# Moving the decay preparation of a recurrence into the stage ahead of it, and half of the output weights to the head of their stage's load queue

## What is computed

```python
f = lb + (1.0 - lb) * jax.nn.sigmoid(hf)                # decay of each token and channel
o, S = hgrn2_scan(silu(hq), 1.0 - f, hi, log(f), S0)    # query, key, value, log decay
...
b = jnp.cumsum(gc, axis=1)                              # summed log decays of a chunk
inter = einsum('bchk,bhkv->bchv', qc * exp(b), S)
S_new = exp(b_last)[..., None] * S + einsum('bshk,bshv->bhkv', kc * exp(b_last[:, None] - b), ic)
...
h = x + mix @ w_out                                     # mix = [attention heads || HGRN2 heads]
```

## Time and profile before

| | |
|---|---|
| median of 3 runs | 3429.63 us (3428.11 to 3436.2) |
| the profiled execution: its own time | 3433.21 us |
| its span in the profile | 3431.4 us |
| PE busy in the span | 3219.1 us (94%) |
| DVE, ACT, POOL busy | 2492.2 us (73%), 1311.3 us (38%), 1023.5 us (30%) |
| mean granted TensorE clock | 0.96 |

### The profile page before, as it was taken

How to read it: one execution, slowest core, us unless ns; L and a number is a source line. 1 busy time by engine, 2 the same in 40 slices (tenths; PEclk the granted TensorE clock), 3 DMA queues, 4 the chain that set the end, 5 groups by cost and what they waited for, 6 DMA issues and landing times. The chain is left out here.

```text
span 3431.4 us, 54854 instructions
## 1 busy us (share of the span) xinstructions
PE 3219.1 (94%) x20435; PEld 1970.3 (57%) x20435; DVE 2492.2 (73%) x5514; ACT 1311.3 (38%) x2581; POOL 1023.5 (30%) x1076
## 2 busy tenths in 40 slices
PE   7999987698899898999999999996999999999997
PEld 4668652575466554666666666653555555555554
DVE  4222562445423489999999999977988888888887
ACT  3000553321200124677776777743222222222222
POOL 0000000000000003899999999952111111111110
PEclk9999998677999999999999999998999999999998
DMA  3220787422422354878888888899788787787774
GB/s 149 98 98 32 271 297 304 164 88 104 169 65 78 126 186 147 278 276 296 298 295 295 279 284 305 294 348 377 288 293 301 281 305 291 291 297 287 294 289 150
DMA packets 213106, 803.43 MB, mean 234 GB/s; under 512 B 33824, under 2 KB 92320, under 8 KB 169088
## 3 DMA queue, kind: packets, MB, share of 16 engines
q1 hardware_dynamic: 176000, 531.81, 42.5%
q0 software_dynamic: 36864, 268.45, 22.4%
HBM read 665.19 MB, written 201.98 MB: 253 GB/s over the span
## 5 line engine op out<-in xcount | busy, mean ns | idle before, releaser
L1692 PE MATMUL psum<-arena 128*128 128x400 f16 x6144 | 1079.8, 334 | 29.4 <-DVE arena L1740 29.3
L2083 PE MATMUL psum<-arena 128*128 128x400 f16 x6144 | 1048.8, 332 | 25.9 <-DVE arena L2129 25.9
L2083 PEld LDWEIGHTS psum<-arena 128*128 128x128 f16 x6144 | 596.1, 97 | 478.6 <-DVE arena L2129 26.3
L1692 PEld LDWEIGHTS psum<-arena 128*128 128x128 f16 x6144 | 592.6, 98 | 444.7 <-DVE arena L1740 33.6
L1664 POOL TENSOR_SCALAR arena<-arena 128x128 f16<-128x128 f16 x800 | 721.6, 915 | 41.0 <-DVEq L1904 24.2
L116 POOL DMA_INDIRECT arena<-in_experts,arena x256 | 286.3, 1118 | 1131.6 <-DVE arena L149 1040.8
L135 ACT ACTIVATE arena<-arena 128x1 f32<-128x1 f32 x256 | 51.5, 201 | 868.0 <-DVE arena L128 867.7
L149 DVE SCALAR_TENSOR_TENSOR arena<-arena 128x1024 f32<-128x1024 f32 x256 | 331.8, 1296 | 21.3 <-issue 9.6
L2136 DVE TENSOR_TENSOR arena<-arena,psum 128x800 f32<-128x800 f32 x256 | 252.1, 985 | 107.3 <-PE psum L2083 107.3
L128 DVE CUSTOM_DVE_ANT_0 arena<-arena 128x1024 f32<-128x1024 f32 x256 | 312.0, 1220 | 19.0 <-DMA arena<-in_experts,arena 18.0
L1955 ACT ACTIVATE arena<-arena 128x128 f16<-128x128 f16 x800 | 246.0, 388 | 86.9 <-DVE arena L1912 86.2
(11 more groups left out here) (241 smaller groups left out, 3425.0 us busy)
## 6 DMA issues: line engine op xcount, KB each, us to landing
arena<-in_u_feat SPq DMA_DIRECT2D x128, 512.0 KB, 7.0
arena<-in_experts SPq DMA_DIRECT2D x128, 512.0 KB, 5.5
scratch_acts<-arena SPq DMA_DIRECT2D x128, 400.0 KB, 5.3
arena<-scratch_gates SPq DMA_DIRECT2D x32, 1600.0 KB, 8.0
arena<-scratch_acts SPq DMA_DIRECT2D x128, 400.0 KB, 6.6
scratch_gates<-arena SPq DMA_DIRECT2D x48, 1024.0 KB, 8.4
out_k_win_sample<-in_cache_k SPq DMA_DIRECT2D x32, 1022.0 KB, 21.5
out_v_win_sample<-in_cache_v SPq DMA_DIRECT2D x32, 1022.0 KB, 21.3
```

The lines of the kernel that those rows point to most:

```text
L1692: last = pe.matmul(psum[:, 2 * p + k, 0:SLD], w[:, s, q, :], xs[:, q, k * SLD:(k + 1) * SLD], start=q == 0 and w is u_hi and xs is x_hi, s ...
L2083: last = pe.matmul(psum[:, 2 * (n % BANKS) + i, 0:SLD], w[:, s, k, q * P:(q + 1) * P], hs[:, s, k, i * SLD:(i + 1) * SLD], start=k == 0 an ...
```

## The change

1. In attend_sample, DVE gets `center_decays()` behind `normalize(1)`: the middles are first copied to tiles of their own, then the sums are centred in place, carries are made, and the sums are clamped. The carries move to a fixed place at the arena's end.
2. ACT makes exp(-centred) for one head group at a time (tile `falling`, which takes the place of `resets`), DVE multiplies that group's keys (`scale_keys(g)`); two groups ahead of `write_out(0)`, two behind it. `copy_turned(1)` stands between groups 1 and 2. Then ACT makes exp(centred) in place and the carries' exponentials, and DVE scales the queries ahead of `write_out(1)`.
3. In hgrn all of that goes, with its waits: PE starts at once with turning the keys. A new `step_dve` 1 only says that the state sum is zeroed.
4. In hgrn SP issues the half of the output weights right behind the first x tile, without a wait, ahead of the second x tile and the seven window copies.
5. In attend_sample SP issues the bias load behind the keys of the first two sequences.

```diff
@@ hgrn, SP
             load_x(0)
+            sp.dma_start(w_half, x["w_out"][:, 0:4, :]).then_inc(w_half_loaded, 16)
             load_x(1)
             shift = SHIFTS_IN + SHIFTS_ATTEND
             for n in range(shift, SHIFTS - 9):
                 shift_window(sp, x, n, windows_shifted)
-            sp.wait_ge(step_dve, 1)
-            sp.dma_start(w_half, x["w_out"][:, 0:4, :]).then_inc(w_half_loaded, 16)
@@ hgrn, ACT
-            act.wait_ge(step_dve, 1)
-            act.activation(ek, eq, ACT.Exp, scale=-1.0).then_inc(step_act, 1)
-            act.drain()
-            act.activation(eq, eq, ACT.Exp)
-            act.activation(carry[:, :, 1:], carry[:, :, 1:], ACT.Exp)
-            act.activation(carry_s, carry_s, ACT.Exp).then_inc(step_act, 1)
...
+            act.wait_ge(step_dve, 1)
             for n in range(NCH):
@@ hgrn, PE
-            pe.wait_ge(keys_scaled, 1)
...
             pe.wait_ge(turn_copied, 9)
-            pe.wait_ge(step_dve, 2)
@@ hgrn, DVE
+            dve.memset(sum_state[:, 0], 0.0)
+            dve.drain().then_inc(step_dve, 1)
             dve.wait_ge(loaded, 16 * 5)
-            (centring of eq, carries, clamp, key and query scaling: L836 to L862)
@@ attend_sample, SP
-            sp.dma_start(bias, x["bias_sample"]).then_inc(constants_loaded, 16)
...
             load_keys(0)
             load_keys(1)
+            sp.dma_start(bias, x["bias_sample"]).then_inc(constants_loaded, 16)
             sp.wait_ge(new_ready, 9)
@@ attend_sample, DVE
+            def center_decays():
+                mid, mid_s = CH // 2 - 1, ST // 2 - 1
+                chunks = f[:, :, 0:SEQ].rearrange("p g (n c) -> p g n c", c=CH)
+                chunks_s = f[:, :, SEQ:T].rearrange("p g (n c) -> p g n c", c=ST)
+                dve.tensor_copy(middle, chunks[:, :, :, mid])
+                dve.tensor_copy(middle_s, chunks_s[:, :, :, mid_s])
+                dve.drain()
+                for g in range(G):
+                    dve.tensor_tensor(chunks[:, g], chunks[:, g],
+                                      middle[:, g].unsqueeze(2).broadcast_to([P, NCH, CH]), ALU.subtract)
+                    dve.tensor_tensor(chunks_s[:, g], chunks_s[:, g],
+                                      middle_s[:, g].unsqueeze(2).broadcast_to([P, SB, ST]), ALU.subtract)
+                dve.drain()
...
+                dve.tensor_scalar(f, f, 40.0, -40.0, ALU.min, ALU.max)
+                dve.drain().then_inc(decay_dve, 1)
+
+            def scale_keys(g):
+                dve.wait_ge(falling_ready, g + 1)
+                dve.tensor_tensor(k[:, g, :], k[:, g, :], falling, ALU.mult).then_inc(keys_scaled, 1)
...
             normalize(1)
+            center_decays()
+            scale_keys(0)
+            scale_keys(1)
             write_out(0)
+            scale_keys(2)
+            scale_keys(3)
+            dve.wait_ge(rising_ready, 1)
+            dve.tensor_tensor(q, q, f, ALU.mult).then_inc(keys_scaled, 1)
             write_out(1)
             dve.wait_ge(out_done, 2 * H)
+            dve.wait_ge(keys_scaled, G + 1)
@@ attend_sample, ACT
             for silu in silus:
                 act.activation(silu, silu, ACT.Silu)
-            copy_turned(1)
+            act.wait_ge(decay_dve, 3)
+            for g in range(G):
+                if g >= 1:
+                    act.wait_ge(keys_scaled, g)
+                act.activation(falling, f[:, g, :], ACT.Exp, scale=-1.0).then_inc(falling_ready, 1)
+                if g == 1:
+                    copy_turned(1)
             act.drain()
+            act.activation(f, f, ACT.Exp)
+            act.activation(carry[:, :, 1:], carry[:, :, 1:], ACT.Exp)
+            act.activation(carry_s, carry_s, ACT.Exp)
+            act.drain().then_inc(rising_ready, 1)
```

More of the change, by code:

```diff
@@ L48 @@
 BIAS0 = WORDS - SEQ
+CARRY0 = WORDS - 4 * (NCH + 1) - 2 * 4 * SB
 ROWS = 2 * P
@@ L185, in build @@
             "row_slots": at(SLOT0, SLOTS, 2 * D), "row_sums": at(SUM0, 2, D), "x_row": at(XROW0, D),
+            "carry": at(CARRY0, G, NCH + 1),
+            "carry_s": at(CARRY0 + G * (NCH + 1), 2, G * SB).rearrange("p a (g b) -> p a g b", g=G),
             "row_index": at(IDX0, 2, P).bitcast(U32), "row_weight": at(WGT0, 2, P),
@@ L589, in hgrn @@
         k = mix[:, 4:8, :]
-        ek = at(word, G, T); word += GT
+        word += SB * 512
         causal = at(word, P); word += P
@@ L594, in hgrn @@
         hnorm = at(word, 1); word += 1
-        carry = at(word, G, NCH + 1); word += G * (NCH + 1)
-        carry_s = at(word, 2, G * SB).rearrange("p a (g b) -> p a g b", g=G); word += 2 * G * SB
+        carry, carry_s = m["carry"], m["carry_s"]
         state = at(word, 4, G, P); word += 4 * G * P
@@ L603, in hgrn @@
         inv = at(word, G * P); word += G * P
-        assert word <= WORDS, word
+        assert word <= CARRY0, word
         eq = at(F0, G, T)
@@ L610, in hgrn @@
         loaded = sem("hgrn_loaded")
-        step_act = sem("hgrn_act")
         step_dve = sem("hgrn_dve")
-        keys_scaled = sem("hgrn_keys_scaled")
         turn_ready = sem("hgrn_turn_ready")
@@ L811, in _ @@
                           masked[0:NS, g, 0:NS], start=g == 0, stop=False, skip_group_check=True)
-            pe.wait_ge(step_dve, 3)
+            pe.wait_ge(step_dve, 2)
             for g in range(G):
@@ L972, in attend_sample @@
         SLOT = 4 * NKEY
-        assert KT * 512 == SLOT and word + 2 * SLOT <= WORDS
+        assert KT * 512 == SLOT and word + 2 * SLOT <= CARRY0
         slot_words = (word, word + SLOT, F0, F0 + SLOT)
@@ L983, in attend_sample @@
         lbt = at(word, 8, G); word += 8 * G
+        q, carry, carry_s, falling = feat[:, FHQ, :, :], m["carry"], m["carry_s"], resets
+        middle = at(word, G, NCH); word += G * NCH
+        middle_s = at(word, G, SB); word += G * SB
         assert word <= F0 + 8 * T
@@ L986, in attend_sample @@
         decay_dve = sem("decay_dve")
+        falling_ready = sem("falling_ready")
+        keys_scaled = sem("keys_scaled")
+        rising_ready = sem("rising_ready")
         constants_loaded = sem("sample_constants_loaded")
@@ L1134, in sum_decays @@
                 dve.drain()
+            def center_decays():
[11 more added lines that the diff above has]
+                dve.drain()
+                ends, ends_s = chunks[:, :, :, CH - 1], chunks_s[:, :, :, ST - 1]
+                dve.tensor_copy(carry[:, :, NCH], ends[:, :, NCH - 1])
+                dve.memset(carry[:, :, 0], 1.0)
+                dve.tensor_tensor(carry[:, :, 1:NCH], ends[:, :, 0:NCH - 1], middle[:, :, 1:NCH], ALU.add)
+                dve.tensor_copy(carry_s[:, 0], middle_s)
+                dve.tensor_copy(carry_s[:, 1], ends_s)
+                dve.drain()
+                dve.tensor_scalar(f, f, 40.0, -40.0, ALU.min, ALU.max)
[3 more added lines that the diff above has]
+                dve.tensor_tensor(k[:, g, :], k[:, g, :], falling, ALU.mult).then_inc(keys_scaled, 1)
             def add_bias(r):
```

## The result

The changed kernel takes 3403.2 us (median of 4 runs, 3397.81 to 3404.84) against 3429.28 us before (4 runs): a ratio of 0.9918, 95% interval 0.9902 to 0.9934, so 26.1 us less where 27.8 were forecast, and inside the range. The profiled execution took 3404.84 us with a span of 3403.1, 28.3 us under the span before; the forecast for it was 3405.4.

The account below looks back on a forecast made before the run. The bound was taken to be a serial chain of load, DVE, ACT, DVE ahead of PE at hgrn's head. Chain 27.4 plus bias 0.4 made 27.8 us, off 3429.6: 3401.8 us, range 3392.9 to 3412.4.

Parts of the forecast that it names:

- The serial chain: Head of hgrn: PE no longer waits for scaled keys and starts turning at about 593.3 instead of 620.67, 27.4 us less.
- The masking: Head of hgrn, DVE: masking due at 605.5, with the five loads landing at 603.53, 2.0 us ahead.
- The output weights: hgrn: load issued at about 604.0 lands at 612.5, 5.7 us ahead of the first half mix; cost nothing.
- rival 2: hgrn: copies share DMA engines with the output weights, first half mix stalls 17 us; gain 10.8, 3418.8 us; chance 0.07.
- The cover in attend_sample: Added DVE and ACT work hides in idle time: 2.2 us to spare before write_out(0), 2.6 before write_out(1).
- The bias load: attend_sample: bias behind the first keys lets scores start up to 2.2 us earlier; gain between 0 and 2.2, 0.4 taken.
- Rival 4: hgrn's recurrence: TensorE's clock runs slower without the rest ahead of it, +92 us in all, 3522 us; chance 0.03.
- the clock's phase: Range term for hgrn's half-mix bursts of 3.76 or 1.97 us: four tiles falling otherwise, 3.6 us either way.

Follow-up runs that it names:

- e1: The kernel after, with hgrn's output-weight load issued behind both x tiles and the seven window copies: 3422.96 us, ratio 0.9991 to the kernel before.
- e4: The kernel after, with all four key scalings and exps ahead of write_out(0) and copy_turned(1): 3403.83 us, ratio 0.9934 to the kernel before.
- e6: The kernel after, with the sample bias loaded ahead of the keys again: 3402.03 us, ratio 0.9929 to the kernel before.

## Why the prediction was right

*The serial chain.* Right, in place and size. The 28.3 us of the span are, in order: attend_sample's end 0.17 earlier (593.24 to 593.07); turning right after the barrier, 27.38 (the wait of 27.43 is now 0.05); turning itself 0.33 shorter (7.82 to 7.49, L719 to L731); 0.43 less from there to the first half mix; then 1.06 lost in the recurrence (212.0 to 213.06) and 1.05 won back behind hgrn. That is the 27.4 of the sum and five small terms that cancel to 0.9. Later stages kept the gain. That the span hits the forecast so closely is in part luck: both profiled executions have five slow bursts, and with three in the one after, the spans would have differed by some 5 us more (an estimate from the lengths in the table).

*The masking.* Due at 605.5, it came at 604.62; the loads had landed by 603.17. Right, though the margin shrank to 1.4 us.

*The output weights.* Right: forecast to land at 612.5 with 5.7 us to spare, they landed at 611.7 with 5.7. e1, which puts the copies ahead, shows what the delay of rival 2 costs: 17.5 us of stall, for the 17 of that rival. Behind the load the copies didn't hold it up: it took 8.1 us, the state's load 8.3. The Trainium skill ("DMA: Bandwidth & Descriptors", section "Queues, rings and completion order") has a ring's descriptors taken in order, and the trace agrees; its warning that a later transfer may finish first decided nothing here.

*The cover in attend_sample.* Right: DVE was free at 566.5 (566.8 forecast) and waited 2.08 us for PE (2.2). e4 shows that this cover is what made it free.

*The bias load.* The weakest term: 0.4 was taken, the stage ended 0.17 earlier in the profiled pair, and e6 shows no gain. A gain of 0 and one of 0.4 can't be told apart, since the stage differs by about 1 us from execution to execution. The scores did start 2.0 us earlier, and the share at 520 to 522 us rose from 0.79 to 1.08, but PE then waited 3.02 us for the next keys: the loads pace that stage.

*The clock.* Rival 4 is out: the recurrence's grant is 0.77 to 0.79 with rests from 2 to 29 us. Why it is no higher, with PE busy for nine tenths, no run here shows. The 3.6 us that the range has for the clock's phase were said to be four tiles, but four times 3.76 - 1.97 is 7.2, so they are two. Lengths from 207.6 to 213.3 us occur, 4.4 below and 1.3 above the 212.0 of the profiled execution before: downwards the term was too small.

## What to carry to other kernels

Look for preparation at the head of a stage that needs only what the stage ahead already has; if an engine idles there, its idle rows give the room, and past it the delay can be passed on in full, as in e4. When a chain is shortened, work out what was hidden behind it: here a load with 10 us to spare became one that is 17 us late, and an edit that is worth nothing alone was needed to keep the gain. Don't expect an earlier first load to help where the sum of the loads sets the pace. Before a chain is moved, see what it waits for: here 10.2 of its 27.4 us were loads that it never read.

## What the runs showed of the hardware that was not expected

The recurrence, the same instructions each time, takes one of several lengths, from 207.6 to 213.3 us at mean grants of 0.79 to 0.77, and the length goes with how many of its eight prompt tiles begin their half mix at a granted clock of 0.50: three, four or five in the thirteen profiled executions. Two executions of one kernel differ in it by 2.1 us. It isn't the rest ahead of it that chooses, and a shift of the start isn't needed for it; what does stays open. Some us of any comparison of this kernel by single profiles are of this kind.

In e4, 3.53 us of idling cost PE more than themselves: the eight turnings behind them ran at a granted clock of 0.50 and took 1.91 us instead of 1.04.
